# Router logits with stationary weights in natural column order, bf16 parts made through PSUM, and a first gather from 64 selection columns

## The reference

```python
x = x + gt1[:, None, :] * (merged @ w_o[l])
h2 = modulate(rmsnorm(x, norm2_g[l]), sh2, sc2)          # rmsnorm * g * (1 + sc2) + sh2
x = x + gt2[:, None, :] * hier_moe(h2, rg_w[l], rg_b[l], re_w[l], re_b[l],
                                   exp_w1[l], exp_w3[l], exp_w2[l])
return rmsnorm(x, final_g)
# in hier_moe
pg = softmax(ht @ rg_w + rg_b); pg_top, g_idx = top_k(pg, 1)
le = (ht @ re_w + re_b) of the chosen group; pe_top, e_idx = top_k(softmax(le), 2)
order = jnp.argsort(a_exp)                               # token-expert pairs sorted by expert
return (jax.nn.silu(xblk @ w1[e]) * (xblk @ w3[e])) @ w2[e]
```

## Time and profile before

| | |
|---|---|
| median of 3 executions | 1885.11 us (1883.81 to 1886.62) |
| profiled execution, its own time | 1884.63 us |
| its span, first to last instruction | 1882.8 us |
| TensorE, VectorE, ScalarE, GpSimd busy | 1758.7, 904.1, 394.9, 17.1 us |
| mean granted TensorE clock | 0.971 |
| read from HBM | 639.20 MB, 341 GB/s over the span |
| end of the w_o product, start of pass 0's first product | 868.7, 914.59 us |

### The profile page before, as it was taken

How to read it: one execution, slowest core, us unless ns; L and a number is a source line. 1 busy time by engine, 2 the same in 40 slices (tenths; PEclk the granted TensorE clock), 3 DMA queues, 4 the chain that set the end, 5 groups by cost and what they waited for, 6 DMA issues and landing times.

```text
span 1882.8 us, 26033 instructions
## 1 busy us (share of the span) xinstructions
PE 1758.7 (93%) x10270; PEld 1010.0 (54%) x10270; DVE 904.1 (48%) x1075; ACT 394.9 (21%) x465; POOL 17.1 (1%) x9
## 2 busy tenths in 40 slices
PE   1979999999999999998799999999999999999996
PEld 1868747786777777686434333343343433333341
DVE  5877766866757644446533333333233332323333
ACT  3010023432323233334111101111010111101011
POOL 0000000000000000001100000000000000000000
PEclk9989999999999999998899999999999999999998
DMA  9996596878868834554499999999999999999994
GB/s 374 386 387 238 208 379 261 325 280 333 326 265 302 312 138 175 190 193 164 199 422 422 422 422 422 422 422 422 422 422 422 422 421 422 422 422 422 422 422 185
DMA packets 140700, 641.92 MB, mean 341 GB/s; under 512 B 12658, under 2 KB 12786, under 8 KB 80114
## 3 DMA queue, kind: packets, MB, share of 16 engines
q1 hardware_dynamic: 139952, 637.08, 84.9%
q10 hardware_dynamic: 562, 2.55, 0.4%
q0 software_dynamic: 144, 1.70, 0.2%
HBM read 639.20 MB, written 2.10 MB: 341 GB/s over the span
## 4 chain that ended last, share of the span: by engine, by line
PE 51%; DMA 38%; DVE 8%; issue 1%; ACT 1%; SPq 1%; DVEq 0%; ACTq 0%
DMA ring<-in_exp_w 33%; PE ps L887 10%; PE ps L657 5%; PE ps L658 5%; PE ps L659 5%; PE ps L627 5%; DVE r_m L1174 4%; PE ps L851 3%; PE ps L570 3%; PE ps L583 3%; DMA ring<-in_branch_w 2%; DMA ring<-in_ada_w 2%; PE ps L752 1%; PE ps L753 1%; PE ps L754 1%; PE ps L874 1%
## 5 line engine op out<-in xcount | busy, mean ns | idle before, releaser
L887 PE MATMUL ps<-ring 128*64 128x512 f32 x2048 | 465.3, 596 | 16.9 <-DMA ring<-in_exp_w 16.9
L887 PEld LDWEIGHTS ps<-ring 128*64 128x64 f32 x2048 | 144.7, 137 | 303.6 <-issue 303.4
L1524 DVE TENSOR_TENSOR r_h<-r_h,ps 128x1024 f32<-128x1024 f32 x128 | 150.5, 1218 | 218.6 <-PE ps L874 218.5
L658 PE MATMUL ps<-g_lo,h_hi 128*128 128x512 f32 x512 | 202.4, 395 | 0.0
L1497 DVE TENSOR_TENSOR r_c<-ps,scale 128x512 f32<-128x512 f32 x65 | 44.7, 688 | 296.2 <-PE ps L829 296.2
L1100 ACT ACTIVATE r_m<-ps 128x512 f32<-128x512 f32 x32 | 19.1, 597 | 712.4 <-PE ps L887 712.4
L657 PE MATMUL ps<-mix_hi,h_hi 128*128 128x512 f32 x384 | 158.5, 413 | 0.0
L1027 ACT ACTIVATE mix_hi<-ring 128x1024 fp32r<-128x1024 f32 x96 | 101.7, 1062 | 260.6 <-PE ps L659 260.6
L1281 DVE TENSOR_TENSOR g_lo<-ring,mix_hi 128x1024 fp32r<-128x1024 f32 x96 | 117.5, 1225 | 79.5 <-ACT mix_hi L1027 78.2
L659 PE MATMUL ps<-mix_hi,h_lo 128*128 128x512 f32 x384 | 152.1, 396 | 0.0
L874 PE MATMUL ps<-ring,r_m 64*128 64x512 f32 x512 | 127.5, 615 | 1.4 <-DVE ring L1517 1.0
(11 more groups left out here) (242 smaller groups left out, 1749.2 us busy)
## 6 DMA issues: line engine op xcount, KB each, us to landing
ring<-in_exp_w SPq DMA_DIRECT2D x320, 1024.0 KB, 22.8
ring<-in_w_in SPq DMA_DIRECT2D x40, 2048.0 KB, 9.9
r_b<-in_exp_w SPq DMA_DIRECT2D x64, 1024.0 KB, 24.4
ring<-in_ada_w SPq DMA_DIRECT2D x24, 2048.0 KB, 18.8
ring<-in_ada_w SPq DMA_DIRECT2D x48, 1024.0 KB, 5.1
ring<-in_w_o SPq DMA_DIRECT2D x8, 2048.0 KB, 7.6
ring<-in_w_in SPq DMA_DIRECT2D x12, 1024.0 KB, 14.9
ring<-in_branch_w SPq DMA_DIRECT2D x6, 2048.0 KB, 9.6
```

What stands on the lines that cost most here:

```text
L658: mm(ps[:, b + t, :], h, lo[:, cols], start=False, stop=False)
L887: last = mm(ps[m * NWIN:(m + 1) * NWIN, 2, :], xe[:, k, :], chunk(2 * c + m)[:, kk * F:(kk + 1) * F], start=(k == 0), stop=(k == KT - 1))
L1524: V.tensor_tensor(x1n, x1n, ps[:, (6, 4)[b]:(6, 4)[b] + 2, :].rearrange("p b n -> p (b n)"), ALU.add).then_inc(added, 1)
```

## The change

- **Router logits.** The router weights come from the host as one array in natural channel order, with 2304 contiguous bytes per partition. They are padded to 64 columns (`rws`) and become the stationary operand, x1T the moving one; even chunks accumulate in PSUM partitions 0 to 63, odd ones in 64 to 127. Transposes of x1 go block by block behind `x1_ready`, the products block by block behind the copies. One more small product with two stacked identities adds the halves and turns the logits back. As scale and shift exist only in `(p k)` order, a new constant and two products (`fan`, in `sum_ada`) make them in natural order too (`tall`).
- **bf16 parts.** xn2 is not stored. ScalarE writes the high part from x1 with the scale. TensorE makes the remainder in PSUM: diag(1/rms) times x1, less the high part (a product with minus identity, `first_rest`); ScalarE saves it as the middle part; TensorE subtracts that in the same bank (`second_rest`); ScalarE saves the low part. GpSimd has no arithmetic left.
- **First gather.** `sel`'s first 64 columns are made first and gather(0) of pass 0 reads `sel` itself; the other 448 follow behind `modulated(0, 1)`, and ScalarE waits for them (`sel_full`). The pass table is saved ahead of `modulated(0, 1)`.
- **Order elsewhere.** Scaling of the router weights and `diag2` stand between w_lo pieces; the counts precede the position products; gt2's row product stands behind the splitting. All four w2 pieces of expert 0 are loaded without a wait for the table, and fgrow behind the last expert's w2. Squares are taken in halves, into `junk`.

```diff
-            sp.wait_ge(parts_sub, 4)
-            sp.wait_ge(parts_act, 4)
-            sp.wait_ge(logit_done, 2)
-            sp.dma_start(fgrow, ...)
-            for q in range(2, 4):
-                load_w2(0, q)
...
+            sp.dma_start(fgrow, ...)
             for t in range(TT):
                 sp.wait_ge(fin_ready, t + 1)
...
+                if SH2 + g == GT2:
+                    pe.wait_ge(fan_ready, 1)
+                    for i in range(2):
+                        last = mm(ps[:, 6, 32 + i * KT:32 + (i + 1) * KT], fan[:, i, :, :], keep[:, K_OCT:K_OCT + KT],
+                                  start=True, stop=True)
...
+                for k in range(4 * n, 4 * n + 4):
+                    side = k % 2
+                    last = mm(ps[side * NWIN:(side + 1) * NWIN, t, 0:P], rws[:, k, :], x1T[:, k, t * P:(t + 1) * P],
+                              start=(k < 2), stop=(k >= KT - 2))
+            def first_rest(t, b, bank):
+                if b == 0:
+                    pe.wait_ge(inv_ready, 3 + t)
+                    pe.wait_ge(hi_ready, t + 1)
+                mm(ps[:, bank, :], root_diag[t], x1_k[:, t, 4 * b:4 * b + 4, :], start=True, stop=False, ...)
+                mm(ps[:, bank, :], minus, xparts[:, 0, t, b * MIX:(b + 1) * MIX], start=False, stop=True, ...
+                   ).then_inc(rest_one, 1)
+            def second_rest(t, b, bank):
+                pe.wait_ge(mid_ready, 4 * t + b + 1)
+                mm(ps[:, bank, :], minus, xparts[:, 1, t, b * MIX:(b + 1) * MIX], start=False, stop=True, ...
+                   ).then_inc(rest_two, 1)
...
             pe.sem_inc(comb_done, 4)
-            pe.wait_ge(sel_ready, 1)
-            pe.wait_ge(parts_sub, 4)
-            gather(0)
+            pe.wait_ge(all_sel, 1)
+            pe.wait_ge(cnt_ready, 2)
...
+            pe.wait_ge(lo_ready, 8)
+            gather(0, sel)
...
+            for b in range(4):
+                part_mid(0, b, 4 + b)
+            for b in range(2):
+                part_mid(1, b, 2 + b)
+            for b in range(4):
+                part_low(0, b, 4 + b)
+            for b in range(2, 4):
+                part_mid(1, b, 2 + b)
+            for b in range(4):
+                part_low(1, b, 2 + b)
...
-            for half in range(2):
-                modulated(0, half)
+            modulated(0, 0)
             v.wait_ge(pass_done, 1)
...
             v.sem_inc(table_ready, 1)
+            modulated(0, 1)
+            one_hot(NWIN, PAIRS)
+            v.sem_inc(sel_full, 1)
```

More of the change, by code:

```diff
@@ L470, in _ @@
             sp.wait_ge(y_done, 16)
-            for q in range(2):
+            for q in range(4):
                 load_w2(0, q)
@@ L921, in _ @@
             pe.wait_ge(xe_ready, 1)
-            gather(1)
+            gather(1, sel)
             first(0, False)
```

302 lines of the change are left out of this document (190 added, 112 removed).

## The result

The changed kernel takes **1869.37 us** (median of 5 executions, 1867.87 to 1872.05) against 1885.11; the ratio is 0.9918 with a 95% interval of 0.9907 to 0.9929. A second series, beside the last experiments, gave 1870.53 us and 0.9925 (0.9911 to 0.9938). The forecast was 1864.6 us with a range of 1858 to 1876: the direction and the range held, and a quarter of the expected gain did not come. Both medians lie above 1868, outside the forecast case (1860 to 1868, given 0.60) and inside two others, dearer splitting or low clock (0.21) and a starving stream (0.08). The profiled execution is the slowest of its five, 1872.05 us, with a span of 1870.3 us.

The account below looks back on a forecast made before the run. The weight stream was taken to bound the loop's second half. Starting it 21.5 us earlier, less charges of 0.4 and 0.6, gave -20.5 from 1884.63, so 1864.1, plus 0.5 for the median: 1864.6 us, range 1858 to 1876.

Parts of the forecast that it names:

- forecast case: The whole kernel's time falls within 1860 to 1868 us; chance 0.60.
- dearer splitting or low clock: Ahead of the first gather, TensorE's strided passes cost more or its clock stays low: 1868 to 1878 us; chance 0.21.
- starving stream: At the loop's start too few weight pieces are queued, losing up to 7.46 us: 1868 to 1873 us; chance 0.08.
- step 6: Weight stream at the loop's start: quarter 0 takes 3.6 us, expert 1's w13 issues at 903.8, not 925.3, gaining 21.5.
- The charge of 0.4 for the start of the stream: Loop start: 0.4 us off the gain, as expert 1's eight pieces must last until pass 1; tightest margin 1.5 us.
- Step 1: End of the w_o product: with VectorE operations moved among earlier w_lo pieces, x1 is complete at 870.3, 2.8 us earlier.
- Step 2: Router logits with stationary weights: ready at 879.9 instead of 888.27, taking 0.11 us a pass for the first 3.5 us.
- Step 3: From last logits to mask: without GpSimd's four operations, VectorE's 7.23 us shrink to 4.75, mask at 884.7.
- Step 4: Splitting products on TensorE ahead of the gather: 0.43 us a strided pass, 1.07 a first_rest, selection ready at 890.5.
- the splitting is dearer: Strided pass costs ScalarE's 0.95 us: quarter 0 starts at 906.4, time about 1871; chance 0.21 together with low clock.
- Step 5: First gather waits for the last low part, starting at 893.4, 15.3 us earlier; VectorE's shorter selection hides behind this.
- rival with a low clock: All the stretch before the loop at 1.2 GHz: issue between 911 and 917, 1871 to 1878 us; within the 0.21.

Follow-up runs that it names:

- two shared versions: v1_vector_half and v5_vector_three: the changed kernel with part of tile 1's splitting moved from TensorE to VectorE; 1865.69 and 1866.56 us.
- e4_full_selection: The changed kernel with all 512 selection columns made ahead of the first gather, as before; 1871.35 us, ratio 0.9925.
- e7_moving_weights: The changed kernel with router logits in their old form, x1T loaded and 36 columns of router weights moving; 1874.08 us, ratio 0.9939.
- e3b_before_small_pool: The kernel before with GpSimd's four subtractions cut from 2048 columns to 8, not computing the layer; 1876.57 us against 1885.77, ratio 0.9953.
- e9_turn_strided: The changed kernel with transposes taking x1 at a stride of 64 bytes, each tile's waiting for the whole tile; 1870.26 us in a single execution.
- e1_contig: The changed kernel with first_rest's fp32 product reading x1 contiguously instead of at a stride of 64 bytes, output different; 1864.51 us, ratio 0.9885.
- v5_vector_three: The changed kernel with VectorE splitting three of tile 1's four blocks, counts behind the third first_rest, gt2 row ahead of the gather; 1866.56 us, ratio 0.9902.
- e8_counts_first: The changed kernel with the counting products moved ahead, behind the third first_rest; 1870.55 us, ratio 0.9917.
- v1_vector_half: The changed kernel with VectorE splitting two of tile 1's blocks, counts behind the third first_rest, gt2 row behind quarter 0; 1865.69 us, ratio 0.9902.

## Why the prediction was right, and where it missed

- **The bound and the stream** (what bounds, step 6): right. S - I is the same within 1.3 us but in the two shared versions, the DMA share is 1.01 behind I, no hole stands between 915 and 960, and the first wait for a landing comes at pass 13 to 14. The charge of 0.4 for the start of the stream was 1.0 in this profile. Low clock in quarter 0 may be a part of it: e4_full_selection, with the full clock, has 957.5, and most profiles with the low one 958 to 958.5, but e7_moving_weights, with the low one, has 957.6.
- **Step 1** (x1 complete): 870.3 forecast, 872.46 seen, 13.0 us behind W where the forecast had 12.85. Right; the 2.0 us are W's. Of them the fan is 0.45 (charged 0.6 with the VectorE operations), the rest is clock lost at two places upstream, 1.6 us each, less an earlier start: the GT2 sums stand at 646.72 here and at 648.32 before.
- **Step 2** (logits at 879.9): 879.97 seen, 877.95 with W's shift taken off. The new form ran at the lower of the two prices, 0.06 us a record, and the full clock, so 2 us better than I took. That price was borrowed from L887 rightly, since both forms run in pairs. In the kernel before the 0.50 of 874 to 876 was read during tile 1's transposes, behind 2.7 us in which TensorE idled; here 32 transposes follow the w_o product without a gap, and the clock reads 1.00 from 870 to 905. By the Trainium skill, "TensorE: Matmul & The Clock Gate", section "Part 4: PE-mode transpose", transposes do not count as busy time for the full clock in the way that other products do; these 3.66 us of transposes brought no low clock.
- **Step 3** (masks in 4.75 us): 4.87 seen, and no operation above 0.3 us. Right, and e3b_before_small_pool shows that this is the greatest single gain, 7.5 us of G - W. The forecast saw the third stall but expected the wait for start_done to return most of it. There the way from the counts to the operation behind start_done (L1454) fell from 2.24 to 1.00 us, so that wait returned 0.43 of the stall's 1.67.
- **Step 4** (splitting): the step that failed, in one term. A strided fp32 pass costs 0.85 us, not 0.43. The mistake was in the choice of the nearest row: the transposes over the same view load that view, they do not stream it (e9_turn_strided). The price called contiguous, 0.23, was half of a pair of passes that run side by side; a pass without a partner is itself 0.43 contiguous (e1_contig and L708 in the trace of before), which is what I took for the strided one. ScalarE's 0.95, the upper end, was the good row: its doubling (3.80 against 1.91) is TensorE's doubling. Eight first_rest at 2 x 0.42 more make 6.7 us; the other steps came out 1.4 better, so G - W missed by 5.3. This is the rival "the splitting is dearer", given 0.21, and the time is near its 1871. Its own working does not close: with the 8.4 us of step 4 quarter 0 would start at 908.4, not at 906.4, and the time would be about 1873. The Trainium skill, "SBUF — State Buffer", section "Door 1: The DMA port swizzle", has such a penalty without a size; the rows agree for operands that stream (2.0 times on TensorE and ScalarE), less for VectorE (1.05 us for 512 elements over the strided view in v5_vector_three, against 0.75 for the contiguous SCALAR_TENSOR_TENSOR over 512 in the earlier trace rows) and for a loaded operand (196 against 140 ns).
- **Step 5** (gather behind ScalarE's last low part, gt2 row just ahead): the gather was released by TensorE's own queue. The gt2 row ended at 900.6, last of all, not 0.5 before the last copy. That VectorE's shorter selection hides was right (e4_full_selection).
- **Step 6** (quarter 0 in 3.6 us): 5.3 from 906.51 to the issue. The full clock ends there:

```profile
905.00:910.00 5.00, 5.00 (x58) 2.58 (x56) 3.70 (x8) 0.00 (x0) 0.00 (x0) 0.66 0.01 3
```

  The 1.2 GHz level comes after the stretch in which TensorE had small table products and a wait of 0.82 us. Nine of the eleven profiles of this family show it, e4_full_selection and v5_vector_three do not, although e4_full_selection has the same table products and the same wait of 0.82 us; what decides is not shown. I - G is 9.43 with the full clock and 10.6 to 11.1 without. The forecast's rival with a low clock had it in another place.
- **The sum.** In the profile the miss is 8.0 us of span (-12.5 against -20.5): 5.3 from G - W, 0.7 from I - G, 1.4 from W beyond the 0.6 charged, 0.6 from S - I. W is 1.8 to 2.0 us late in both profiles of the changed kernel and lies between 856.99 and 859.91 in its variants, which none of their edits explains, so I count it as chance. The medians, 4.8 us above the forecast (5.9 in the second series), carry mainly the first of these terms.

## What to carry to other kernels

Before taking a row as the price of a matmul, read which operand streams and which is loaded, and whether its neighbours run beside it: the same view cost 4% as the loaded operand (0.113 against 0.109 us) and doubled the time as the streaming one, and a row of fp32 passes over 512 columns showed 0.23 us each where two stood side by side and 0.43 where each stood alone. When a small operation on one engine takes ten times its usual time while another engine streams through memory, try first what taking that stream away gives; here it was most of the gain. A transfer moved out of a queue is worth its bytes only if the queue, and not the slot behind it, is the later of the two.

## What the runs showed of the hardware that I had not expected

- A plain fp32 pass of 512 moving columns takes 0.43 us at the full clock with 128 loaded columns; with 64 loaded columns two passes that write different halves of the PSUM partitions take 0.43 together (L887, 914.59, in the trace of before). With 128 loaded columns over a 64-byte stride a pass takes 0.85.
- The time outside the span was 1.76 to 1.88 us in all 33 executions of the kernel before that ran beside the experiments, but 1.75 to 2.86 in ten of the changed kernel (mean 2.3), and up to 2.98 in e1_contig, e4_full_selection and e8_counts_first, while v1_vector_half and v5_vector_three kept to 1.76 to 1.85. It adds about 0.5 us to the changed kernel's median. What it is stays open.
- The granted clock of single stretches differs from execution to execution of one kernel: from the GT2 sums to the gap near 782 the changed kernel took 136.4 us in one profile and 134.8 in the other. Behind that gap it differs by 1.6 us between variants that have the same code there. A difference of 2 us between two profiles needs these stretches compared first.
